# RMS norms behind matrix products: root and reciprocal of one number per token, spread over the partitions by a matmul with the identity

## The reference

```python
def _rmsnorm(h, g):
    h32 = h.astype(jnp.float32)
    y = h32 * lax.rsqrt(jnp.mean(h32 * h32, axis=-1, keepdims=True) + NORM_EPS)
    return (y * g.astype(jnp.float32)).astype(h.dtype)
...
    for i in range(DEPTH):                       # first stack
        h = _ffn_half(h, norm_g[i, 0], m[:, 0], m[:, 1], m[:, 2], ffn_w_in[i, 0], ffn_w_out[i, 0])
        u = _modnorm(h, norm_g[i, 1], m[:, 3], m[:, 4])
...
        h = h + m[:, 5] * y                      # y: Fourier mixer (i = 0), retention mixer (i = 1)
        h = _ffn_half(h, norm_g[i, 2], m[:, 6], m[:, 7], m[:, 8], ffn_w_in[i, 1], ffn_w_out[i, 1])
    return _rmsnorm(h, final_norm_g)
...
    for l in range(DEPTH):                       # second stack
        f = _swiglu(_rmsnorm_2(h, ff1_norm_pre[l]), ff1_w_gate[l], ff1_w_up[l], ff1_w_down[l])
        h = h + 0.5 * _rmsnorm_2(f, ff1_norm_post[l])
...
        h = h + _rmsnorm_2(m, mix_norm_post[l])
        f = _swiglu(_rmsnorm_2(h, ff2_norm_pre[l]), ff2_w_gate[l], ff2_w_up[l], ff2_w_down[l])
        h = h + 0.5 * _rmsnorm_2(f, ff2_norm_post[l])
```

## Time and profile before

| | us |
|---|---|
| runs before: median of 3 | 2806.75 |
| lowest and highest | 2802.41, 2808.07 |
| the profiled execution | 2814.55 |
| its span, first to last instruction | 2812.5 |
| TensorE matmuls busy | 2733.2 (97%) |
| VectorE busy | 1725.1 (61%) |
| ScalarE busy | 1130.7 (40%) |
| all reciprocals of L1246 (19) | 41.3 |

### The profile page before, as it was taken

The page is one execution under the profiler, slowest core; times in us unless marked ns, Lnnn a source line. Parts: engine busy times, 40 slices in busy tenths (PEclk is TensorE's granted clock), DMA queues, the critical chain, the costliest instruction groups (busy, mean ns, idle before and its releaser), DMA issues. The chain is left out here.

```text
span 2812.5 us, 44245 instructions
## 1 busy us (share of the span) xinstructions
PE 2733.2 (97%) x18354; PEld 2463.0 (88%) x18354; DVE 1725.1 (61%) x2095; ACT 1130.7 (40%) x1405; POOL 0.9 (0%) x13
## 2 busy tenths in 40 slices
PE   7999999999999999999999999999999999999998
PEld 5888878878888888888998999999989999997997
DVE  6773754777325753444446655766876676587765
ACT  5222223422224222225244544544554444454543
POOL 0000000000000000000000000000000000000000
PEclk9999999999999999999999999999999999999999
DMA  8653631456333654544222565566526656652564
GB/s 271 210 181 109 193 113 38 134 180 187 96 94 99 198 186 127 178 136 127 84 91 84 181 185 185 166 210 187 158 62 197 190 165 187 184 169 75 159 192 128
DMA packets 377287, 428.70 MB, mean 152 GB/s; under 512 B 14000, under 2 KB 359344, under 8 KB 377008
## 3 DMA queue, kind: packets, MB, share of 16 engines
q1 hardware_dynamic: 376416, 424.79, 48.8%
q10 hardware_dynamic: 720, 1.74, 0.2%
HBM read 425.43 MB, written 1.05 MB: 152 GB/s over the span
## 5 line engine op out<-in xcount | busy, mean ns | idle before, releaser
L715 DVE TENSOR_TENSOR w_lo<-raw,w_hi 128x1024 fp32r<-128x1024 f32 (+1 forms) x672 | 799.3, 1199 | 818.5 <-ACT w_hi L706 811.8
L1071 PE MATMUL ps<-u_hi,w_hi 128*128 128x256 f32 (+1 forms) x3520 | 1120.4, 318 | 20.2 <-DVE u_lo L1324 6.7
L1073 PE MATMUL ps<-u_hi,w_lo 128*128 128x256 f32 (+1 forms) x3520 | 1111.6, 316 | 0.0
L1072 PE MATMUL ps<-u_lo,w_hi 128*128 128x256 f32 (+1 forms) x3520 | 1111.6, 316 | 0.0
L706 ACT ACTIVATE w_hi<-raw 128x1024 fp32r<-128x1024 f32 (+1 forms) x672 | 690.7, 1035 | 1031.4 <-PE ps L1073 934.0
L1071 PEld LDWEIGHTS ps<-u_hi,w_hi 128*128 128x128 f32 x3520 | 663.3, 188 | 81.4 <-issue 28.5
L1072 PEld LDWEIGHTS ps<-u_lo,w_hi 128*128 128x128 f32 x3520 | 663.5, 188 | 45.8
L1073 PEld LDWEIGHTS ps<-u_hi,w_lo 128*128 128x128 f32 x3520 | 661.6, 188 | 46.4
L1071 PE MATMUL ps<-g_hi,w_hi 128*128 128x256 f32 (+1 forms) x1408 | 450.8, 320 | 0.0
L1073 PE MATMUL ps<-g_hi,w_lo 128*128 128x256 f32 (+1 forms) x1408 | 450.1, 320 | 0.0
L1072 PE MATMUL ps<-g_lo,w_hi 128*128 128x256 f32 (+1 forms) x1408 | 450.1, 320 | 0.0
(11 more groups left out here) (252 smaller groups left out, 1997.3 us busy)
## 6 DMA issues: line engine op xcount, KB each, us to landing
raw<-in_ffn_w_in SPq DMA_DIRECT2D x176, 512.0 KB, 4.4
raw<-in_w_mod SPq DMA_DIRECT2D x128, 512.0 KB, 4.4
raw<-in_ff_w_gate SPq DMA_DIRECT2D x88, 512.0 KB, 4.1
raw<-in_ff_w_up SPq DMA_DIRECT2D x88, 512.0 KB, 4.3
raw<-in_ffn_w_out SPq DMA_DIRECT2D x64, 512.0 KB, 3.5
raw<-in_ff_w_down SPq DMA_DIRECT2D x64, 512.0 KB, 4.3
raw<-in_ret_w_in SPq DMA_DIRECT2D x48, 512.0 KB, 3.7
raw<-in_w_in SPq DMA_DIRECT2D x36, 512.0 KB, 3.7
```

Source lines behind the costliest of these rows:

```text
L715: dve.tensor_tensor(w_lo[:, slot, at], raw[:, raw_slot, 0:cols], w_hi[:, slot, at].bitcast(f32), ALU.subtract).then_inc(lo_ready, 1)
L1071: pe.matmul(out, w_hi[:, slot, cols], hi, start=first, stop=False, **check)
L1072: pe.matmul(out, w_hi[:, slot, cols], lo, start=False, stop=False, **check)
L1073: return pe.matmul(out, w_lo[:, slot, cols], hi, start=False, stop=last, **check)
```

## The change

In the twelve norms behind a product the token sums are turned: the tiles of squares are now the weights and a single column of ones is the moving operand (`pe_token_sums`), so that a sum comes out with tokens on partitions, one column for each 128 tokens. ScalarE and VectorE take root and reciprocal of this [128, 2] or [128, 4] block, `token_root`. TensorE then multiplies each column, broadcast to a 128x128 weight, with the identity `eye` (`pe_spread`), which puts the token's number on all partitions, in bank `STAT` again; the scaling steps read it there in place of `rstd`. The filler moves behind the spread: 12 matmuls in the first stack, 10 in the second. `eye` is loaded once by a DMA on ScalarE's queue behind that of `dft`. The memset of `poolw` moves from ahead of the final norm's scaling to behind its first `u_lo` tile. The buffers laid out behind `eye` move by 512 bytes on each partition.

```diff
@@ -191,7 +191,7 @@
             after = stages[j + 1] if j + 1 < len(stages) else None
             s.holds_last = after is not None and after.kind == "stats" and any(x.kind == "gemm" for x in stages[j + 1:])
         elif s.kind == "stats" and gemm is not None and gemm.squares:
-            s.more["begun"] = True
+            s.more["begun"], s.c["spread"] = True, 1
             if not gemm.holds_last:
                 gemm = None
                 continue
@@ -421,7 +421,9 @@
         root_of_eps = sb("root_of_eps", [P, 1])
         cond = sb("cond", [P, DT, 2])
         eps = sb("eps", [P, 2])
-        overlay_room = sb("overlay_room", [P, 88])
+        eye = sb("eye", [P, P])
+        token_root = sb("token_root", [P, NTOK // P])
+        overlay_room = sb("overlay_room", [P, 84])
 
         _, g_hi, g_lo = overlay([("g_room", [P, 16], f32), ("g_hi", [P, FT, NTOK], f32r),
                                  ("g_lo", [P, FT, NTOK], f32r)])
@@ -509,6 +511,8 @@
         stat_ready = sem("stat_ready")
         root_ready = sem("root_ready")
         rstd_ready = sem("rstd_ready")
+        eye_landed = sem("eye_landed")
+        spread_ready = sem("spread_ready")
         scaled_ready = sem("scaled_ready")
         u_hi_ready = sem("u_hi_ready")
         u_lo_ready = sem("u_lo_ready")
@@ -1232,9 +1236,10 @@
             n = g.more["tokens"]
             act.wait_ge(stat_ready, t["stat"] + 1)
 
-            wide = n + (n // P if g.more.get("by_row") else 0)
+            wide = n // P if g.more.get("begun") else n + (n // P if g.more.get("by_row") else 0)
             four = 4.0 if g.more.get("half") else 1.0
-            act.activation(rstd[:, 0:wide], ps[:, STAT, 0:wide], ACT.Sqrt, scale=four / D,
+            root = token_root if g.more.get("begun") else rstd
+            act.activation(root[:, 0:wide], ps[:, STAT, 0:wide], ACT.Sqrt, scale=four / D,
                            bias=eps[:, 1:2] if four == 4.0 else eps[:, 0:1]).then_inc(root_ready, 1)
             if g.more.get("held"):
                 split_hi(act, g.more["held"], t, 0, RING - 1)
@@ -1242,16 +1247,40 @@
         def dve_stats(dve, g, t):
             n = g.more["tokens"]
             dve.wait_ge(root_ready, t["stat"] + 1)
-            wide = n + (n // P if g.more.get("by_row") else 0)
-            dve.reciprocal(rstd[:, 0:wide], rstd[:, 0:wide]).then_inc(rstd_ready, 1)
+            wide = n // P if g.more.get("begun") else n + (n // P if g.more.get("by_row") else 0)
+            root = token_root if g.more.get("begun") else rstd
+            dve.reciprocal(root[:, 0:wide], root[:, 0:wide]).then_inc(rstd_ready, 1)
+
+        def pe_token_sums(pe, source, n, begins, ends):
+
+            for tb in range(n // P):
+                ins = pe.matmul(ps[:, STAT, tb:tb + 1], source[:, tb * P:(tb + 1) * P], ones[:, 0:1],
+                                start=begins and tb == 0, stop=ends, skip_group_check=True)
+            return ins
+
+        def pe_tail_stats(pe, g, t):
+            n = g.more["tokens"]
+            pe.wait_ge(sums_ready, t["sum"])
+            pe_token_sums(pe, acc[:, 0, :], n, True, False)
+            for b in range(2):
+                pe.wait_ge(squares_ready, t["sq"] - 1 + b)
+                ins = pe_token_sums(pe, tmp1[:, b, :], n, False, b == 1)
+            ins.then_inc(stat_ready, 1)
+
+        def pe_spread(pe, g, t):
+
+            if t["spread"] == 0:
+                pe.wait_ge(eye_landed, 16)
+            pe.wait_ge(rstd_ready, t["stat"] + 1)
+            for tb in range(g.more["tokens"] // P):
+                ins = pe.matmul(ps[:, STAT, tb * P:(tb + 1) * P], token_root[:, tb:tb + 1].to_broadcast([P, P]),
+                                eye[:, :], start=True, stop=True)
+            ins.then_inc(spread_ready, 1)
 
         def pe_stats(pe, g, t):
-            n, tail = g.more["tokens"], g.more.get("begun")
+            n = g.more["tokens"]
             pe.wait_ge(sums_ready, t["sum"])
-            ins = pe.matmul(ps[:, STAT, 0:n], ones[:, :], acc[:, 0, 0:n], start=True, stop=not tail)
-            for b in range(2 if tail else 0):
-                pe.wait_ge(squares_ready, t["sq"] - 1 + b)
-                ins = pe.matmul(ps[:, STAT, 0:n], ones[:, :], tmp1[:, b, 0:n], start=False, stop=b == 1)
+            ins = pe.matmul(ps[:, STAT, 0:n], ones[:, :], acc[:, 0, 0:n], start=True, stop=True)
             for tb in range(n // P if g.more.get("by_row") else 0):
                 ins = pe.matmul(ps[:, STAT, n + tb:n + tb + 1], acc[:, 0, tb * P:(tb + 1) * P], ones[:, 0:1],
                                 start=True, stop=True)
@@ -1336,11 +1365,14 @@
 
         def dve_scaled(dve, g, t, k):
             n = g.more["tokens"]
-            if k == 0 and begun(t["stat"]):
+            root = rstd[:, 0:n] if g.more.get("lead") else ps[:, STAT, 0:n]
+            if k == 0 and g.more.get("lead"):
                 dve.wait_ge(rstd_ready, t["stat"])
+            elif k == 0:
+                dve.wait_ge(spread_ready, t["spread"])
             if begun(t["uhi"] + k - 1):
                 dve.wait_ge(u_hi_ready, t["uhi"] + k - 1)
-            dve.tensor_tensor(tmp2[:, k % 2, 0:n], h[:, k, 0:n], rstd[:, 0:n], ALU.mult).then_inc(scaled_ready, 1)
+            dve.tensor_tensor(tmp2[:, k % 2, 0:n], h[:, k, 0:n], root, ALU.mult).then_inc(scaled_ready, 1)
 
         def dve_apply_tile(dve, g, t, k):
 
@@ -1369,13 +1401,12 @@
 
         def dve_post(dve, g, t, gain=None):
 
-            if begun(t["stat"]):
-                dve.wait_ge(rstd_ready, t["stat"])
+            dve.wait_ge(spread_ready, t["spread"])
             for k in range(DT + 2):
                 if k < DT:
                     if begun(t["post"] + k - 1):
                         dve.wait_ge(post_ready, t["post"] + k - 1)
-                    dve.tensor_tensor(tmp2[:, k % 2, 0:SEQ], f_out[:, k, :], rstd[:, 0:SEQ], ALU.mult
+                    dve.tensor_tensor(tmp2[:, k % 2, 0:SEQ], f_out[:, k, :], ps[:, STAT, 0:SEQ], ALU.mult
                                       ).then_inc(post_scaled_ready, 1)
                 if 0 < k <= DT:
                     if begun(t["px"] + k):
@@ -1391,15 +1422,13 @@
 
         def dve_final(dve, g, t, gain):
 
-            dve.memset(poolw[:, :, :], 0.0).then_inc(poolw_zeroed, 1)
             dve.wait_ge(lvec_landed, 16)
-            if begun(t["stat"]):
-                dve.wait_ge(rstd_ready, t["stat"])
+            dve.wait_ge(spread_ready, t["spread"])
             for k in range(DT + 2):
                 if k < DT:
                     if begun(k - 1):
                         dve.wait_ge(post_ready, k - 1)
-                    dve.tensor_tensor(tmp2[:, k % 2, 0:SEQ], h[:, k, 0:SEQ], rstd[:, 0:SEQ], ALU.mult
+                    dve.tensor_tensor(tmp2[:, k % 2, 0:SEQ], h[:, k, 0:SEQ], ps[:, STAT, 0:SEQ], ALU.mult
                                       ).then_inc(post_scaled_ready, 1)
                 if 0 < k <= DT:
                     dve.wait_ge(post_scaled_ready, k)
@@ -1407,6 +1436,8 @@
                                       ALU.mult).then_inc(post_ready, 1)
                 if k >= 2:
                     dve_gain_tile(dve, gain, t, k - 2)
+                if k == 2:
+                    dve.memset(poolw[:, :, :], 0.0).then_inc(poolw_zeroed, 1)
                 if k == 5:
                     dve_held(dve, g, t)
 
@@ -2165,6 +2196,8 @@
 
                         act.wait_ge(unit_used, t["unit"])
                         act.dma_start(dft[:, :, :], T["dft"]).then_inc(dft_landed, 16)
+                        act.dma_start(eye[:, :], T["tables2"][:, TWO_AT["ident"]:TWO_AT["ident"] + P]
+                                      ).then_inc(eye_landed, 16)
                     stream(act, g, t, follower(whole, j), split_hi, act_evacuate, act_stats, act_tail)
                     if g.name == "q":
                         act_first_decays(act)
@@ -2270,8 +2303,9 @@
                 elif isinstance(g, Gemm):
                     pe_gemm(pe, g, t)
                 elif g.kind == "stats" and t["startup"]:
-                    pe_stats(pe, g, t)
-                    pe_keep_busy(pe, t, 6.0 if g.more["tokens"] == NTOK else 4.0)
+                    pe_tail_stats(pe, g, t)
+                    pe_spread(pe, g, t)
+                    pe_keep_busy(pe, t, 2.6)
                 elif g.kind == "startup":
                     pe_startup(pe, t)
                 elif g.kind == "fourier":
@@ -2281,9 +2315,10 @@
                 if isinstance(g, Gemm):
                     pe_gemm(pe, g, t)
                 elif g.kind == "stats":
-                    pe_stats(pe, g, t)
+                    pe_tail_stats(pe, g, t)
+                    pe_spread(pe, g, t)
                     if follower(second, j) is not None:
-                        pe_keep_busy(pe, t, 4.0)
+                        pe_keep_busy(pe, t, 2.2)
                 elif g.kind == "mixer":
                     pe_mixer(pe, t, g.more["layer"])
                 t.add(g)
```

## The result

The changed kernel takes 2815.05 us (median, 2804.39 to 2824.80) where the kernel before takes 2802.84 beside it (2793.13 to 2808.07, 20 runs each): 1.0044 times as long, 95% interval 1.0034 to 1.0054. It is slower, by 0.44%. The forecast was 2790.7, range 2780 to 2801, with 0.05 on slower. The profiled execution took 2817.22 us.

The account below looks back on a forecast made before the run. TensorE, busy 97% of the span, was taken as the bound, with time won where norms leave it no product. Savings of 9.32 + 1.56 + 3.80 + 0.39 + 0.99 = 16.1 us took 2806.75 to 2790.7, range 2780 to 2801.

Parts of the forecast that it names:

- The sum of the norms: Savings at the twelve norms behind a product, added over all places: 16.1 us.
- Root: ScalarE's root in the norms, on 2 or 4 columns: about 0.26 us in place of 0.47 or 0.69.
- reciprocal: VectorE's reciprocal in the norms: 0.16 us, 0.21 with hand-over, against 1.75 and 3.35; named as the gain.
- spread: New matmuls broadcasting the token's number: 0.79 us at 256 tokens, 1.24 at 512; upper-bound rival 6.2 us more, chance 0.06.
- scaling from PSUM: VectorE's scaling steps reading PSUM cost nothing extra; the rival that they do: 2791.7 us, chance 0.03.
- filler binding: Behind the retention product (1577), filler ends last, so the product starts 0.39 us earlier, of the chain's 0.99.
- the final norm of the first stack: Final norm at 1770: the stage gains 0.99 us, its first tile comes 1.39 early.
- 2090 and 2607: Two 256-token norms with the tail just in time: 0.78 us won at each, 1.56 together.
- The base: Starting time: profiled execution 2814.55 us, 7.8 over the median 2806.75 of the runs shown, from which 16.1 was taken.
- The rival on the clock: TensorE's short waits at eleven norms halve its clock, 1.7 us each: 2809.4, priced at 2828.1; chance 0.05.
- The rival on the pace: Restarts redraw the pace of five 256-token stages: one slow 2797.2, one fast 2784.3; chances 0.17 slow, 0.11 fast.
- The sign: Whole kernel against before: faster 0.87, the same within 0.2% 0.08, slower 0.05.

Follow-up runs that it names:

- e16: Changed kernel with token sums moving 128 columns of ones, buffers placed as in e14: 2864.53 us, 1.0187 of the kernel before.
- e1: Kernel before with only 32 bytes more in overlay_room, moving g_hi and the buffers behind it: 2827.87 us, 1.0063 of the kernel before.
- e6: e1 again on a second chip, the kernel before with g_hi and the buffers behind it moved 32 bytes: 2834.63 us, 1.0078.
- e7: The changed kernel without an edit, measured again on a second chip: 2819.31 us, 1.0023 of the kernel before.
- e15: Changed kernel with its one-column sums, buffers placed as in e14: 2865.13 us, 1.0185 of the kernel before.
- e3: Changed kernel with g_hi back on a multiple of 128 and sums moving 128 columns of ones: 2799.45 us, 0.9971; repeated later, 2792.21 us, 0.9921.
- e5: Changed kernel, buffers as the change left them, with token sums moving 128 columns of ones: 2814.71 us, 1.0016 of the kernel before.
- e2: Changed kernel with overlay_room 16 bytes smaller, g_hi back on a multiple of 128, one-column sums kept: 2802.02 us, 0.9967 of the kernel before.
- e14: Kernel before with u_hi and g_hi placed 32 bytes past a multiple of 128 and the weights on one: 2881.29 us, 1.0245.

## Why the prediction was wrong

*The sum of the norms held.* Root 0.262 us (0.26), reciprocal 0.154 to 0.180 (0.16), spread 0.75 and 1.24 (0.79 and 1.24), scaling from PSUM free,'s filler binding (0.44 to 0.55 won for 0.39). Where no pace is drawn the change is worth 16.2 us, forecast 16.1. That the two are so close is in part luck: at full clock the norms win more than forecast (1.26 us for 0.99 at the final norm of the first stack, 0.9 to 1.07 for 0.78 at 2090 and 2607), 16.8 in e16, and the clock takes some of it back. The base was taken from one profiled run, 2814.55, and three runs; 20 runs of before gave 2802.84, and that run lies above all of them. From there the norms alone would have come to 2786.7.

*What failed is a step that was left at nothing: the move of the buffers.* The text ahead of the prediction has it (as 512 bytes, when it was 544), and the prediction prices every instruction that the change adds and none of the addresses that it moves. 32 more bytes between g_hi, g2_hi, ret_hi and the weights cost: 3 wide down products x 3.5 = 10.4 us; five narrow ones, 528 matmuls each, from 113.3 ns or 117.8 by chance to 118.3, which is 2.6 or 0.3 us, 7.3 for the five with half of them fast; less than 2 for the products on ret_hi. Some 19 us together; e1 and e6 measured 14.5 and 25.3 between medians. 19 less 16.2 is 3 us slower. The change measured 12.2 slower on its own comparison, with an interval of 9.5 to 15, and 6.5 by its ratio in e7. What lies between is as large as the clock's loss in the traces: the changed kernel's gaps are 7.3 us shorter and its last norm 1.1, and 19 less 8.4 is 11 slower; for e7 it is 19 less 10.2, 9 slower. But the medians of e15 and e16 show only 0.6 of such a loss, so the clock's share is not settled. And the kernel before took 2802.84 in this comparison and 2809.36 to 2814.17 in the four others, which no run explains.

*The rival on the clock was half right.* "The clock falls: slower than before" had 0.05 and the reason against it was that each new wait is under 1.21 us with filler between them. The wait wasn't alone: ahead of it stand 12 or 24 passes of one column. The earlier trace rows had that very form of pass and I read its duration there, not what it does to the clock. The Trainium skill, "TensorE: Matmul & The Clock Gate", section "A second HAM failure mode: psum-queue depth-cycling", tells of a kernel whose frequent short idle times between groups of matmuls made the clock swing. Here waits of that kind alone did not do it: e3 and e16 have them at the same places (0.76 us ahead of the spread in e16's row), and their clock falls at no norm. The price, 1.7 to 3.4 us at each of eleven, was too high: 0.6 to 2.3 us at those caught, four to eight in a run. It didn't decide the sign; e5, without it, is still 1.0016.

*The rival on the pace was right as a source of scatter* (28 fast of 50, 6 to 7 us a stage) and said nothing of its cause. Had it asked on which pairs of operands the two paces occur, it might have led to addresses.

*The sign.* The change as built is slower by its side effect; with 16 bytes less of room it is faster: e2 0.9967, e3 0.9971 and 0.9921 on two chips. e3 is the version to keep. Its 16 us of shorter gaps are in every trace with wide sums, and these sums leave the clock alone.

Open: what in the chip makes the distance matter, what sets a pace at a restart, which of the norms with narrow sums are caught, and how much they cost on average (0.6 us or 4.6 by medians, 4.4 to 8.6 by the gaps of the traces).

## What to carry to other kernels

A change that adds a buffer moves every buffer behind it: compare the addresses of the built programs, and where a stage far from the change slows by a constant ns for each matmul, ask for the distance of its operands before anything else; and take it from what the instruction reads, not from where the buffer starts. To measure a few us in a kernel with a two-valued pace, first make a base in which the pace is fixed, even a slower one; there five runs of each kernel told what twelve had not. And a passage made of tiny matmuls is short in time, but the work behind it may find TensorE's clock at half.

## What the runs showed of the hardware

- Start to start, a 512-column fp32r matmul takes 226.7 ns when what it reads as moving operand lies at distance 0 from its weights, modulo 256 bytes; 233.3 at 32 and at 224, 234.3 at 160, 228.9 at 64. With 256 columns: 120.0 at 0 and 96, 118.3 at 224, 117.3 or 118.7 at 160, 113.3 or 117.8 by chance at 192. Modulo 128 they fit less well: 234.3 and 233.3 (160 and 32), 120.0 and 118.3 (96 and 224) would each be one distance. With these products moved off 0 and 192 (e14) the kernel loses 2.45%.
- A pace once drawn holds for the rest of the stage, up to some 1500 matmuls and from one product into the next at distance 192, until TensorE is interrupted; 0.2 us in place of 0.11 from start to start was enough at 1599.79 of the changed kernel.
- The spread (data broadcast as weights, identity moving, 128 columns, fp32) costs 0.11 us a pass, 1.24 us to VectorE for 512 tokens, both at full clock.
- Passes with one moving column before a wait of 0.65 us were followed by a clock of 0.50 at four to eight of twelve norms in a run; passes with 128 columns in the same places were not, in any of the seven traces that have them. Both take about as long (first weights to root 3.11 us at 503.79 in the changed kernel, 3.22 at 499.10 in e3).
